# One more bias matmul per wide attention piece, in place of the bias column of its two sigmoids, from the end of the gates on

## The reference

```
z[t,s]  = q_t . k_s / sqrt(64) + bias_h
A[t,s]  = sigmoid(z[t,s]) * prod_{s<j<t} (1 - sigmoid(z[t,j]))
out_t   = sum_s A[t,s] v_s
```

## Time and the profile before

| | us |
|---|---|
| median of 3 runs | 1894.5 (1893.62 to 1896.02) |
| the profiled execution | 1892.12 |
| its span in the profile | 1890.4 |
| attention past the gates' end, in the span | about 1536 to 1781 |

### The profile page before, as it was taken

One profiled execution on the slowest core, in us unless ns is written; L12 is line 12 of the kernel. 1 busy time (PEld: TensorE's weight loads), 2 busy tenths in 40 slices (PEclk: granted clock), 3 DMA queues, 4 the chain that ended last, 5 costly groups with the idle time before them and its releaser, 6 DMA issues. The chain is left out here.

```text
span 1890.4 us, 27863 instructions
## 1 busy us (share of the span) xinstructions
PE 1809.5 (96%) x10103; PEld 1426.2 (75%) x10103; DVE 1055.5 (56%) x1975; ACT 811.1 (43%) x1682; POOL 81.2 (4%) x140
## 2 busy tenths in 40 slices
PE   5999999999999999999999999999999988999998
PEld 2678787878787878677778767888777766676677
DVE  4563535353535353624446345755278788888852
ACT  3742323232323332313345223433367677878620
POOL 2000000000000000000000000011000000000000
PEclk8899999999999999999999999999999999999999
DMA  9221212130304040583424663224313353553252
GB/s 324 84 93 58 92 57 93 55 113 35 126 22 139 10 148 5 189 273 100 134 56 176 204 216 105 82 92 127 111 46 82 79 172 95 157 152 128 57 178 95
DMA packets 184938, 215.53 MB, mean 114 GB/s; under 512 B 45352, under 2 KB 142560, under 8 KB 183809
## 3 DMA queue, kind: packets, MB, share of 16 engines
q1 hardware_dynamic: 171146, 167.17, 28.9%
q0 software_dynamic: 13696, 47.08, 6.5%
HBM read 165.39 MB, written 48.83 MB: 113 GB/s over the span
## 5 line engine op out<-in xcount | busy, mean ns | idle before, releaser
L475 PE MATMUL rt_acc<-rt_w_hi,rt_h_hi 128*128 128x512 f32 x504 | 203.4, 403 | 1.0 <-DVE rt_h_lo L1014 1.0
L477 PE MATMUL rt_acc<-rt_w_hi,rt_h_lo 128*128 128x512 f32 x504 | 197.2, 391 | 0.0
L476 PE MATMUL rt_acc<-rt_w_lo,rt_h_hi 128*128 128x512 f32 x504 | 196.5, 390 | 0.0
L1057 DVE TENSOR_TENSOR rt_by_cos<-rt_raw,rt_cos 128x256 f32<-128x256 f32 (+1 forms) x72 | 30.5, 424 | 243.9 <-ACT rt_raw L887 243.9
L898 ACT COPY rt_qk_t<-rt_tr 128x256 f32<-128x256 f32 (+1 forms) x72 | 26.0, 361 | 278.4 <-PE rt_tr L706 278.4
L2943 PE MATMUL kq_acc<-kq_w_hi,kq_h 128*128 128x512 f32 x320 | 127.1, 397 | 0.0
L2944 PE MATMUL kq_acc<-kq_w_lo,kq_h 128*128 128x512 f32 x320 | 124.7, 390 | 0.0
L2946 PE MATMUL kq_acc<-kq_w_hi,kq_h 128*128 128x512 f32 x320 | 124.7, 390 | 0.0
L1937 ACT COPY pa_w_t<-pa_wt 128x512 f32<-128x512 f32 (+2 forms) x160 | 86.8, 543 | 73.4 <-PE pa_wt L1755 70.6
L2050 DVE TENSOR_TENSOR_SCAN pa_after_key<-pa_keep 128x128 f32<-128x128 f32 (+3 forms) x128 | 101.8, 815 | 19.8 <-ACT pa_take L1919 8.7
L477 PEld LDWEIGHTS rt_acc<-rt_w_hi,rt_h_lo 128*128 128x128 f32 x504 | 94.6, 188 | 20.6
(11 more groups left out here) (414 smaller groups left out, 4167.5 us busy)
## 6 DMA issues: line engine op xcount, KB each, us to landing
ro_a_raw<-retained SPq DMA_DIRECT2D x14, 1024.0 KB, 5.9
op_ada<-in_ada_w SPq DMA_DIRECT2D x8, 1024.0 KB, 13.1
rt_w_raw<-in_ret_w_in SPq DMA_DIRECT2D x16, 512.0 KB, 5.0
rt_w_raw<-in_ret_w_in SPq DMA_DIRECT2D x8, 1024.0 KB, 7.8
rt_old<-in_state_ret SPq DMA_DIRECT2D x8, 1024.0 KB, 5.9
rt_g_raw<-in_ret_w_in SPq DMA_DIRECT2D x8, 1024.0 KB, 5.2
out_st_sample<-rt_new POOLq DMA_DIRECT2D x8, 1024.0 KB, 8.0
kq_w_raw<-in_sb_w_in SPq DMA_DIRECT2D x4, 2048.0 KB, 8.8
```

What stands on the lines that cost most here:

```text
L475: nc.tensor.matmul(dst, h_hi[:, k, cols], w_hi[:, k, :], start=k == 0, stop=False)
L476: nc.tensor.matmul(dst, h_hi[:, k, cols], w_lo[:, k, :], start=False, stop=False)
L477: last = nc.tensor.matmul(dst, h_lo[:, k, cols], w_hi[:, k, :], start=False, stop=k == KD - 1)
```

## The change

The test for who gets the bias matmul, so far "two heads in the piece", becomes "a prompt piece with two heads, or any prompt piece behind `G_END`". For those pieces PE issues the matmul of L1743, and ACT the two sigmoids without a bias column.

```diff
+        def shifted(p):
+
+            return pieces[p].b is None and (len(pieces[p].heads) == 2 or p > G_END)
...
                 for i, hh in enumerate(at.heads):
                     dst, keys = z[:, p % 2, i * n:(i + 1) * n], k_t[:, pair % 2, hh, c0:c0 + n]
                     nc.tensor.matmul(dst, q_hi[:, g % 2, hh, at.u % QG, :], keys, start=True, stop=False)
-                    if len(at.heads) == 2:
+                    if shifted(p):
                         head = 2 * pair + hh
                         nc.tensor.matmul(dst, share[:], bias_parts[:, head:head + 1].to_broadcast([P, n]), start=False, stop=False)
...
                 dst, src = (keep[:, p % 2, 0:n], take[:, p % TR, 0:n]), z[:, p % 2, 0:n]
-                if len(at.heads) == 2:
+                if shifted(p):
                     nc.scalar.activation(dst[0], src, ACT.Sigmoid, scale=-(DH ** -0.5))
                     nc.scalar.activation(dst[1], src, ACT.Sigmoid, scale=DH ** -0.5).then_inc(sticks, 1)
```

## The result

The median is 1900.72 us (8 runs) against 1894.08 for the kernel before (8 runs). The ratio is 1.0029, with a 95% interval of 1.0020 to 1.0038: +5.5 us, between +3.8 and +7.2. The forecast was +4.5.

What follows compares the result with a forecast made beforehand. A chain through PE, ACT and DVE was taken to bound the attention. Between its floor of +3.2 (5.5 - 2.3) and a count of +5.6 by PE's waits, +4.5 was chosen: 1894.5 + 4.5 = 1899.0 us, range 1893.0 to 1905.5.

Steps and rivals of the forecast that it cites:

- Three engines, none full, so a chain sets the pace: From 1549 to 1777 us, PE, DVE and ACT are each 81 to 91% busy; a chain passing between them sets the pace.
- the rival of a cheaper matmul: The added matmul costs less than its neighbours: +1 us, about 1895.5; chance 3%.
- The 131 ns: Skill's spacing for a 512-column matmul in a stream with weight loads; by it the chain would add an estimated +1.0 us.
- The floor of +3.2: Along the chain from 1549 to the last weights: scores on PE +5.5 us, sigmoids on ACT -2.3; others can only be longer.
- The list of sigmoids: On the chain's ACT stretches: 26 sigmoids with a column, each 0.09 us faster, -2.3 us together.
- The second count: By PE's 35 late starts, 1549 to 1777: waits absorb 8.8 of 14.4 us, leaving +5.6, or +3.8 after DVE's cover.
- what DVE hides at the end: In the last 45 us DVE sets the time; 1.8 us of added PE work goes into PE's wait before the end.
- What I set at nothing: Four changed wide pieces before 1549 cost nothing, PE waiting there anyway; without that cover 0.9 us.
- PE becomes the bound all through: Rival: PE's extra 14.4 us falls outside its waits, +8 to +14, about 1905; chance 13%.
- The waits take in nearly all: Rival: PE's waits absorb nearly all the added work, 0 to +3, about 1896.5; chance 14%.
- ACT's relief wins: Rival: faster sigmoids and longer scores close all PE's late starts, 18.6 us, giving about -4, 1890.5; chance 7%.
- The clock dip goes away: Rival: the lower clock at 1576 to 1578, costing at most 1.7 us, vanishes: +2.8, about 1897.3; chance 8%.

Runs made afterwards that it cites:

- the halves: Against the kernel before: extra matmul with the sigmoids' bias column kept, stretch +7.10 us, ratio 1.0034; only the bias column dropped, stretch -2.95 us, ratio 0.9986.
- The 27 pieces: The change in only the 27 wide pieces whose score the prediction counted on its chain, against the kernel before: stretch +4.77 us, ratio 1.0026.
- the other 47: The change in only the remaining 47 wide pieces past the gates, against the kernel before: stretch -0.59 us, ratio 0.9992.
- the six pairs: The change in only wide pieces 75, 84, 85, 87, 106 and 111, against the kernel before: stretch +0.04 us, ratio 0.9999.
- a second one: The changed kernel with the bias matmul issued twice in wide pieces past the gates, against the kernel before: stretch +14.57 us, ratio 1.0074.
- the second heads: The change in only the 37 wide pieces past the gates holding a pair's second head, against the kernel before: stretch +3.72 us, ratio 1.0005.

## Why the prediction was right

**The views.** "Three engines, none full, so a chain sets the pace" held. Between the two extremes, PE's 14.4 us in full and nothing, the halves measured +7.1 and -2.95, and the whole +5.04; with the dip counted alike, +6.7, -1.9 and +4.8.

**The prices.** 0.22 for 512 columns and 0.09 a sigmoid, as taken from the earlier trace rows. So the rival of a cheaper matmul is out. The 131 ns from the Trainium skill's "TensorE: Matmul & The Clock Gate", section "Back-to-back issue gap", are not what this stream does; its other figure, 216 ns for an isolated matmul of 512 columns, is within the spread of 0.214 to 0.217 from the new matmul to its follower, measured after in all 56.

**The chain.** The floor of +3.2 held (5.04), and so did its parts: at least 5.5 for the matmuls (7.1 measured, 6.7 with the dip as before), no more than 2.3 for the sigmoids (1.9, without the dip). The 27 pieces that I had counted on it carry +4.2, the other 47 +0.5 (both with the dip as before). This is shown by experiment. The list of sigmoids on it was wrong: of the six pairs that were to lie on it without their score, five gave nothing. From piece 83 to 92 DVE is as full as ACT, and faster sigmoids of pieces 84, 85 and 87 give nothing; nor does the score of piece 90 cost more than 0.05 us in the kernel with the 27. That DVE is the reason fits the timeline and was not tested by itself. For 106 and 111 the reason is open. That is ten of the 26, 10 x 0.09 = 0.9 us of relief too much in the sum.

The trace of before, followed back once more by the semaphore updates and not by which row ended last, shows the same fault. It has 26 of the 27 scores (not that of 83) and those of 76, 88 and 112, 21 of 512 and 8 of 384; but only 14 sigmoids, the pairs of pieces 73, 82, 93, 101, 118, 138 and 146, and none of the six. Its sum is 21 x 0.22 + 8 x 0.165 - 14 x 0.09 = +4.7 us, against +4.83 with the dip as before. It was read after the result, and it is not exact either: it allows the faster sigmoids 1.3 us by themselves, and they gave 1.9.

**The second count.** 5.6 less what DVE hides at the end, 3.8, was nearer to the +5.04 before the correction than after it, though the correction is right in itself: the tail costs 0.25 to 0.31. So the count by PE's waits took in too much elsewhere, by about 1.2 us. It let each wait swallow up to 0.40 by itself. I think that it fails where two waits of one round draw on the same relief, which I didn't test: this is not shown.

**What I set at nothing.** The four wide pieces ahead of 1549: in the changed kernel the weights of pieces 60 and 66 stand to those of 71 as before, within 0.01 us.

**The forecast.** +4.5 against +5.04 in the stretch and +5.5 (3.8 to 7.2) in the whole. The mechanism held, and the size is in part luck: 4.5 was a choice between 3.2 and 5.6, not a sum, and what it added to the floor (1.3) made up for 0.9 of relief that was not there.

**What the profile was to show.** 74 rows of the new matmul, spacing and sigmoids as said. PE +11.6 in the stretch, under "12 to 14"; ACT -10.9, where I said 13 (the rows overlap, so less of it shows as busy time). ACT's wait for turned weights +17.8, as said (13 and the growth of the stretch). DVE without a break in the last 30 to 45 us: nearly. At 1777.45 it waits 0.15 for sigmoids, and the PE share rose there, so that PE now works as long as DVE in the tail (43.4 and 42.2 of the 45 us from 1741 to 1786).

**The rivals.** "PE becomes the bound all through" did not come true with one matmul; of a second one, two thirds are paid. "The waits take in nearly all" is refuted by the +5.04 and by the 27 pieces. "ACT's relief wins" is refuted by its half: the faster sigmoids give 2.95 us with the lost dip and 1.9 without it, and the matmuls alone cost 7.1. "The clock dip goes away" did not happen here (6.46 us between the scores), but did in two other kernels; in the kernel before it cost 1.07 of the 1.7 that were set as the most. With the change it became 0.2 dearer.

## What to carry to other kernels

Where several engines are 80 to 90% busy, the sum of an engine's work tells little; follow the chain back from the end and count how many of the changed instructions lie on it. It gives a floor that held here. An instruction behind a hand-over was nearly free and the same one before it was paid: 27 pieces cost 4.2 us, 47 others 0.5. Go by who updated the semaphore: where two engines both work without a break, the rows alone put sigmoids on the chain that were not on it. And measure between two landmarks inside the profile: this stretch repeated to 0.06 us, when runs of one kernel lie 4 to 10 us apart. See first whether the granted clock falls inside it, and count that apart.

## What the runs showed of the hardware that was not expected

The granted clock fell to 0.50 (1.2 GHz, the lower of its two levels) for some 3 us near piece 80 in all kernels but two, always behind the same pause of PE, and its price can be read off: the scores of pieces 80 and 82, with narrow pieces between them that are identical in all kernels, are 5.18 us apart without it and 6.24 to 6.78 with it, more the earlier it begins. One dip so costs 1.07 to 1.60 us. It went away with the faster sigmoids alone, in two profiles of two, and with the change in the 47 pieces beside the chain, though PE does not stand less ahead of it: its wait for the low part of q before piece 80 is 1.65 us (1.64 in two) with the dip and without it. In the second heads a second dip appeared. What decides between them stays open; that a small shift in rhythm can add or take 1 us by the clock alone is what the rows show. "TensorE: Matmul & The Clock Gate" of the Trainium skill, section "What's actually happening", has idleness bring the lower clock; the rows agree that a pause comes first, and show that the same pause doesn't always do it.
